# The prologue of a two-layer encoder trunk: more of the first adaLN sums on TensorE, GpSimd's rotary angles earlier, nine more idle products

## The reference, cut to what matters

```python
mod = (c @ w + b)[:, None, :]                  # w is 1024 x 3072
shift, scale, gate = jnp.split(mod, 3, axis=-1)
u = x * (1.0 + scale) + shift
proj = u @ w_in                                # first product of the mixer
...
inv_freq = ROPE_THETA ** (-jnp.arange(0, ROT_DIM, 2) / ROT_DIM)
ang = positions[..., None] * inv_freq          # rotary tables
cos, sin = jnp.cos(ang), jnp.sin(ang)
```

## Time and profile before

| | us |
|---|---|
| median of 3 executions | 2107.39 |
| lowest and highest | 2107.19, 2108.32 |
| the profiled execution's own time | 2107.35 |
| its span, first to last instruction | 2105.4 |
| TensorE busy in the span | 2070.4 (98%) |
| VectorE, ScalarE, GpSimd busy | 1189.1 (56%), 1025.9 (49%), 1406.3 (67%) |
| mean granted TensorE clock | 0.996 |

### The profile page before, as it was taken

The page is one execution under the profiler, slowest core; times in us unless marked ns, Lnnn a source line. Parts: engine busy times, 40 slices in busy tenths (PEclk is TensorE's granted clock), DMA queues, the critical chain, the costliest instruction groups (busy, mean ns, idle before and its releaser), DMA issues.

```text
span 2105.4 us, 27351 instructions
## 1 busy us (share of the span) xinstructions
PE 2070.4 (98%) x9619; PEld 1701.4 (81%) x9619; DVE 1189.1 (56%) x1945; ACT 1025.9 (49%) x1834; POOL 1406.3 (67%) x1773
## 2 busy tenths in 40 slices
PE   7999999999999999999999999999999999999997
PEld 6877778787888888888788888888778888888887
DVE  5888888575515554777632545687651454333235
ACT  3585356555516674374633656234552464433332
POOL 4987767856677887875567885564546776545554
PEclk9999999999999999999999999999999999999999
DMA  8654545533434354553233333332323232434332
GB/s 300 157 134 147 160 128 147 163 110 101 120 110 124 107 162 145 140 159 94 75 105 100 118 103 93 99 106 71 101 73 108 87 104 83 128 100 128 93 93 78
DMA packets 421508, 250.06 MB, mean 119 GB/s; under 512 B 48149, under 2 KB 393085, under 8 KB 421373
## 3 DMA queue, kind: packets, MB, share of 16 engines
q1 hardware_dynamic: 420506, 248.03, 40.1%
q10 hardware_dynamic: 867, 0.29, 0.1%
HBM read 242.71 MB, written 4.26 MB: 117 GB/s over the span
## 4 chain that ended last, share of the span: by engine, by line
PE 80%; POOL 8%; DVE 4%; ACT 4%; issue 3%; DMA 1%; SPq 0%; POOLq 0%; ACTq 0%; DVEq 0%
PE fg L862 25%; PE fg L864 25%; PE fg L863 25%; POOL w_lo L1884 4%; POOL ada_acc L1955 1%; PE bank_s L948 1%; DVE bank_c L1496 1%; ACT ada L1283 1%; DMA stage_in<-in_x_dram 1%; PE bank_l L874 1%; PE bank_t L970 1%; PE bank_l L885 1%; PE bank_t L957 0%; ACT w_hi L1127 0%; POOL ssum L1978 0%
## 5 line engine op out<-in xcount | busy, mean ns | idle before, releaser
L1884 POOL TENSOR_TENSOR w_lo<-raw,w_hi 128x256 fp32r<-128x256 f32 (+1 forms) x1425 | 1032.3, 756 | 626.7 <-ACT w_hi L1127 625.2
L862 PE MATMUL fg<-u_hi,w_hi 128*128 128x512 f32 x2112 | 838.6, 397 | 5.8 <-DVE u_lo L1476 2.1
L864 PE MATMUL fg<-u_hi,w_lo 128*128 128x512 f32 x2112 | 823.7, 390 | 0.0
L863 PE MATMUL fg<-u_lo,w_hi 128*128 128x512 f32 x2112 | 823.4, 390 | 0.0
L1127 ACT ACTIVATE w_hi<-raw 128x1024 fp32r<-128x1024 f32 (+2 forms) x387 | 375.6, 970 | 386.5 <-PE fg L864 282.9
L862 PEld LDWEIGHTS fg<-u_hi,w_hi 128*128 128x128 f32 x2112 | 397.0, 188 | 103.9 <-issue 16.2
L864 PEld LDWEIGHTS fg<-u_hi,w_lo 128*128 128x128 f32 x2112 | 397.0, 188 | 84.6
L863 PEld LDWEIGHTS fg<-u_lo,w_hi 128*128 128x128 f32 x2112 | 397.4, 188 | 81.8 <-issue 2.6
L1496 DVE SCALAR_TENSOR_TENSOR bank_c<-glu,par,bank_c 128x512 f32<-128x512 f32 x448 | 306.1, 747 | 0.1
L1838 DVE SCALAR_TENSOR_TENSOR x<-fg,mod,x 128x512 f32<-128x512 f32 (+1 forms) x168 | 121.6, 724 | 320.0 <-PE fg L864 319.8
L864 PE MATMUL fg<-h_hi,w_lo 128*128 128x512 f32 (+1 forms) x704 | 269.8, 383 | 0.0
(11 more groups left out here) (264 smaller groups left out, 1846.2 us busy)
## 6 DMA issues: line engine op xcount, KB each, us to landing
raw<-in_w_up_dram SPq DMA_DIRECT2D x176, 512.0 KB, 3.8
ada<-in_w_ada_ffn_dram SPq DMA_DIRECT2D x48, 512.0 KB, 4.5
raw<-in_w_down_dram SPq DMA_DIRECT2D x64, 384.0 KB, 3.4
raw<-in_w_in_dram SPq DMA_DIRECT2D x40, 512.0 KB, 3.9
raw<-in_w_down_dram SPq DMA_DIRECT2D x64, 320.0 KB, 3.1
ada<-in_w_ada_mix_dram SPq DMA_DIRECT2D x32, 512.0 KB, 4.3
raw<-in_w_in_dram SPq DMA_DIRECT2D x32, 256.0 KB, 3.8
raw<-in_w_out_dram SPq DMA_DIRECT2D x32, 256.0 KB, 2.9
```

The lines of the kernel that those rows point to most:

```text
L862: pe.matmul(out, hi[:, k, :], rhi, start=k == order[0], stop=False)
L863: pe.matmul(out, hi[:, k, :], rlo, start=False, stop=False)
L864: ins = pe.matmul(out, lo[:, k, :], rhi, start=False, stop=k == order[-1])
L1884: ins = pool.tensor_tensor(lo_of(n)[:, ks, :], raw[n % NRAW][:, ks, :], hi_of(n)[:, ks, :].bitcast(F32), ALU.subtract)
```

## The change

Three things are changed, all in the prologue.

1. For the pieces 4 to 8 (chunks 1 and 3) two row tiles, k = 6 and 7, are summed by TensorE, and six instead of seven by VectorE.
2. The constants with the frequencies get a semaphore of their own (in_freq), and GpSimd's angles wait for that one and the positions. GpSimd's order becomes: the common steps, the whole first table and the first three steps of the second, `split_lo(0)`, eight steps of the second table, `split_lo(1)`, `first_lo` of four tiles, the last two steps, `split_lo(2)`, the wait for set_pe, the `glu` memsets, the memsets of `kz`, `v_t` and `swapped`, and then `split_lo(3)`.
3. Nine idle products stand in `first_rest` between `first_sums(1)` and the wait for the parameter rows.

```diff
-FIRST_ON_PE = [range(DT - 1, DT) for _ in FIRST_PIECES]
+FIRST_ON_PE = [range(DT - (1 if p < TB else 2), DT) for p in range(len(FIRST_PIECES))]
...
-                                          start=(o, i) == (0, 0), stop=False)
+                                          start=(o, i, k) == (0, 0, FIRST_ON_PE[p][0]), stop=False)
...
             def first_rest():
                 pe.wait_ge(fold_step, FOLDED["half", 0])
                 first_sums(1)
+                idle_products(9, bank_s)
                 pe.wait_ge(in_taps, 16 * 2 * DEPTH)
...
+            pe.wait_ge(in_freq, 16)
             pe.wait_ge(in_const, 16 * IN_CONST)
...
-            load(const[:, P:], a["consts"][:, P:])
+            act.dma_start(const[:, P:], a["consts"][:, P:]).then_inc(in_freq, 16)
...
-            for n in range(2):
-                split_lo(n)
+            angles()
+            whole_turns(0)
+            for n in range(len(TWO_PI)):
+                less_turns(0, n)
+            clamped(0)
+            whole_turns(1)
+            split_lo(0)
+            for n in range(len(TWO_PI)):
+                less_turns(1, n)
+            split_lo(1)
             for k in range(DT // 2):
                 first_lo(k)
-            angles(0)
+            clamped(1)
             split_lo(2)
             pool.wait_ge(set_pe, 4)
             for j in range(CT):
                 history(0, j)
-            angles(1)
-            split_lo(NHI)
             pool.memset(kz[:], 0.0).then_inc(kv_hist, 1)
             pool.memset(v_t[:, 0:CHUNK], 0.0).then_inc(kv_hist, 1)
             for buf in swapped:
                 pool.memset(buf[:], 0.0).then_inc(swap_clear, 1)
+            split_lo(NHI)
```

More of the change, by code:

```diff
@@ L66 @@
     _n += _c
-IN_CONST = 1 + len(ROWS1)
+IN_CONST = len(ROWS1)
 def conv_slabs(l, b, tiles):
@@ L584, in build @@
         tr_done, t_copied, pv_done, ahi, alo = (sem(n) for n in ("tr_done", "t_copied", "pv_done", "att_hi", "att_lo"))
+        in_freq = sem("in_freq")
         in_const, in_taps, in_sinks, in_pos, tab_out = (sem(n) for n in ("in_const", "in_taps", "in_sinks", "in_pos", "tab_out"))
@@ L1893, in step_, with angles, whole_turns, less_turns @@
                 pool.wait_ge(angle_step, steps[0])
[L1895 to L1911, removed]
+            def angles():
+                pool.wait_ge(in_freq, 16)
+                pool.wait_ge(in_pos, 16 * HALF)
+                step_(pool.tensor_copy(ang[:], pos[:]))
+                step_(pool.tensor_scalar(ang[:], ang[:], inv_freq, None, ALU.mult))
+            def whole_turns(i):
+                step_(pool.tensor_scalar(turns[:], ang[:], float(np.float32(0.5 / np.pi)), (0.25, 0.0)[i], ALU.mult, ALU.add))
+                step_(pool.tensor_scalar(turns[:], turns[:], MAGIC, None, ALU.add))
+                step_(pool.tensor_scalar(turns[:], turns[:], -MAGIC, None, ALU.add))
+            def less_turns(i, n):
+                step_(pool.tensor_scalar(whole[:], turns[:], -TWO_PI[n], None, ALU.mult))
+                step_(pool.tensor_tensor(tabs[i][:], whole[:], (tabs[i] if n else ang)[:], ALU.add))
+            def clamped(i):
+                step_(pool.tensor_scalar(tabs[i][:], tabs[i][:], (np.pi / 2, 0.0)[i], PI_DOWN, ALU.add, ALU.min))
+                step_(pool.tensor_scalar(tabs[i][:], tabs[i][:], -PI_DOWN, None, ALU.max))
             def history(mi, j):
```

## The result

The changed kernel takes 2112.36 us (median of 12 executions, 2110.34 to 2115.48), the kernel before 2107.23 in the same comparison (2105.80 to 2109.11). The ratio is 1.0025, with a 95% interval of 1.0016 to 1.0034: slower by 5.1 us, 3.4 to 7.2. I had forecast 2106.5 with a range of 2105.4 to 2109.3. The profiled execution took 2111.84 us, with a span of 2109.8; before it was 2107.35 and 2105.4.

The account below looks back on a forecast made before the run. The prediction took TensorE as the bound from 51 us to the end. Its terms, +1.58 + 0.2 - 0.3 - 2.33 = -0.85 us, took 2107.35 to 2106.5 us, range 2105.4 to 2109.3.

Parts of the forecast that it names:

- What bounds the kernel, and that slab 0's end is passed on: After 51 us TensorE bounds the kernel, so slab 0's end shifts the kernel's end nearly one to one.
- Part 1, +1.58 us: Second sums: 16 added one-column instructions on TensorE, 0.79 us for eight, add 1.58 us, bounds 1.2 to 1.8.
- if the clock holds: Slab 0's second half: at the full clock it takes 5.0 us instead of 7.33; forecast's chance 0.46.
- the fall behind the sums: Clock falls as the second sums end at 42.0, idle instructions run at 0.242 us each: +1.3, 2108.7 us; chance 0.32.
- Rival B: Clock falls inside the second sums: one-column instructions cost 2.4 us more, idle ones 2.2, up to +4.5, 2111.9; chance 0.05.
- -0.85: Sum of the forecast's terms at slab 0's end, +1.58 + 0.2 - 0.3 - 2.33 us.
- Part 2: GpSimd's earlier angles delay the first product by 0.2 us (0 to 0.7); u_lo stands 2.3 us after the sums, not 3.49.
- Part 3, 2.19 us and -2.33: Behind the second sums 18 idle instructions take 2.19 us; the second half starts 0.3 sooner and takes 2.33 less.

Follow-up runs that it names:

- the second looks: One more execution each, unchanged, of the kernel before, the changed kernel and the kernel with 20 idle products: 2105.38, 2112.46 and 2117.19 us.
- the kernel with 20 idle products: The changed kernel with 4, 4, 5, 7 idle products in and behind the second sums and the memsets late: 2112.42 us, ratio 1.0031.
- part 3 alone: The kernel before with only nine idle products added behind the second sums: 2106.31 us, ratio 0.9999.
- parts 2 and 3: The changed kernel with the old one row tile on TensorE instead of two: 2105.44 us, ratio 0.9997.
- part 1 alone: The kernel before with only the second row tile of chunks 1 and 3 moved to TensorE: 2111.18 us, ratio 1.0024.
- part 2 alone: The kernel before with only GpSimd's new order and the semaphore in_freq: 2106.83 us, ratio 0.9999.

## Why the prediction was wrong

**What bounds the kernel, and that slab 0's end is passed on:** right in direction for the two kernels compared, and in size partly by luck. +3.79 at the tanh became +4.4 in the span, over a dip and two longer waits. In the second looks +4.27 at the tanh became +6.9: the lag is 3.4 us at the tanh of 107 us, 5.2 at that of 257, 6.2 behind the wait for h_lo at 780, and the last 0.7 arises behind 2057 us. For the kernel with 20 idle products it did not hold.

**Part 1, +1.58 us:** the work was sized rightly, 16 instructions in 1.68 us while the clock was full. The time was not. The sums took 4.54 us longer, of which 3 are clock. The step that failed is "if the clock holds", on which the forecast's -2.33 and the 2.19 for the idle products both rest: I gave it 0.46, gave the fall behind the sums 0.32 and the fall inside the sums 0.05, on the ground that the sums of before were not throttled at 38 to 40. That was one execution, in which the clock fell at 41.8, just behind the sums. Two kernels with the old one row tile show falls at 39.8 (part 3 alone) and 40.3 (parts 2 and 3), inside them. The added instructions are not needed for the fall, which comes without them as well; they lengthen the stretch in which it comes, and those behind the fall take twice their time. What ends the low stretch is not shown: in both profiles of the changed kernel the clock was back (49.3, 49.6) just before the first product of 512 columns (49.75, 49.70), behind idle products, while in part 1 alone it came back at 51.8, 4.5 us after such products had begun. Rival B was what happened. My price of up to +4.5 was its 2.4 and 2.2 us alone, without the forecast's own terms; -0.85 + 2.4 + 2.2 is +3.75, and +3.79 came out at the tanh, with 3.0 for the 2.4 and 1.9 for the 2.2. The +5.1 of the median holds more than the prologue.

**Part 2:** the angles' 18 steps started at 10.81 and ended at 18.5 (forecast 11.7 and 19.5), `split_lo(1)` started at 26.15 (25.9), the first product at 30.30 (30.2), slab 2's low weights took 2.77, and u_lo stood 2.0 us behind gain. That was right for the changed kernel, where TensorE's late transposes held the memsets back until 49.6. I had written of the memsets only that their leaving a later place gains nothing, and had not asked what they meet in the new one: in part 2 alone they cost 0.8 us at the second half's start, 0.3 at the tanh (51.02 against 50.68), and nothing that the time can tell. The Trainium skill, "GPSIMD Engine Reference", section "Specifications", says that GpSimd shares its memory interfaces with VectorE and contends with VectorE instructions of a 2-port mode or with two inputs in that memory. The trace agrees that they slow each other, with 2.69, 1.88 and 1.00 us for the same two instructions; it does not show their mode.

**Part 3, 2.19 us and -2.33:** the second half did take 5.1 us instead of 7.37. But the 18 instructions took 4.05 us, and what they were to protect was lost before they began: the clock had been low for 6 us. Without them the median is 1.8 us lower.

**Busy time and the clock:** in eight of the profiles in the table the clock fell with TensorE and its weight loads both shown fully busy, in or right behind products of one column. Busy time in the profile is thus no sign that the clock will hold. The Trainium skill, "TensorE: Matmul & The Clock Gate", section "HAM oscillation — how this bites in real kernels", puts the fall down to waits between bursts; these eight falls have no such wait just ahead of them, so that account does not cover them.

## What to carry to other kernels

Work for TensorE in products of one column costs its own time and, in most profiles here, also a longer stretch at the lower clock: look at what the clock does in that stretch in more than one profile before adding to it. With idle products inside such a stretch, ahead of the fall, the clock held through the sums in four of five profiles; the fifth, of a kernel with part 1, lost it all the same, and the gain in time without part 1 (1.5 to 2.1 us) is too small to be told. Behind the fall nine idle products took 4.05 us, where the rows of before made them 2.19. When a memset is moved into an idle stretch of GpSimd, ask what VectorE does there.

## What the runs showed that I had not expected

The place at which the clock falls moves from execution to execution of the same program: 41.8 and 40.7 in the kernel before, and in another kernel not at all or at 39.4, worth 6.8 us at slab 0's end. One clean profile is then no proof that a clock is held. And a full-clock prologue that ends in time did not give the time back: with 20 idle products and part 1, 4.9 us of span arose from 0.2 us at 51 us, 2.8 of them 700 us later behind a slower transfer. That transfer is a little or much slower in every profile with part 1, so what a change in the first 50 us costs has to be looked for in the whole trace.
